# Gate and up weights of an expert: one load each, or two half loads, in a two-block model with a 64-expert layer

## The reference

```python
def swiglu(x, wg, wu, wd):
    return (jax.nn.silu(x @ wg) * (x @ wu)) @ wd
...
    _, idx = lax.top_k(jnp.where(emask, sel, -jnp.inf), TOP_K)     # 6 of 64 experts a token
...
    def block(args):
        tok, w, e = args
        y = swiglu(h[tok], w_gate[e], w_up[e], w_down[e])
        return y * w[:, None]
```

## Time and profile before

| | |
|---|---|
| three runs | 2684.3, 2684.98 (median), 2685.8 us |
| the profiled execution | 2684.57 us, of which 2682.8 are the span from the first to the last instruction |
| what lies around the span | 1.8 us |
| expert stage (first `gate_up` to last down product) | 2075.5 to 2653.4 us of the span |
| PE busy over the whole span | 95% |

### The profile page before, as it was taken

The page is one execution under the profiler, slowest core; times in us unless marked ns, Lnnn a source line. Parts: engine busy times, 40 slices in busy tenths (PEclk is TensorE's granted clock), DMA queues, the critical chain, the costliest instruction groups (busy, mean ns, idle before and its releaser), DMA issues. The chain is left out here.

```text
span 2682.8 us, 30830 instructions
## 1 busy us (share of the span) xinstructions
PE 2557.9 (95%) x10865; PEld 1547.2 (58%) x10865; DVE 1061.1 (40%) x2302; ACT 667.0 (25%) x1319; POOL 600.1 (22%) x539
## 2 busy tenths in 40 slices
PE   8999999999999999999999989999999999999994
PEld 7547888445666478874444537666755443444441
DVE  1126887103333266650023335556623322322226
ACT  2224444202333221210035532222112111111111
POOL 3017887200000144521121001101110111111110
PEclk9999999999999999999989999999998999999997
DMA  4235655532221233232232121110125799999997
GB/s 136 79 94 147 178 161 164 127 87 58 57 56 56 63 94 94 78 90 78 67 87 63 42 52 27 27 32 2 39 84 204 303 419 414 402 389 403 394 393 293
DMA packets 292214, 404.57 MB, mean 151 GB/s; under 512 B 14434, under 2 KB 253752, under 8 KB 267520
## 3 DMA queue, kind: packets, MB, share of 16 engines
q1 hardware_dynamic: 275136, 366.18, 39.6%
q0 software_dynamic: 15632, 34.44, 4.0%
q10 hardware_dynamic: 1328, 2.38, 0.2%
HBM read 396.20 MB, written 27.71 MB: 158 GB/s over the span
## 5 line engine op out<-in xcount | busy, mean ns | idle before, releaser
L947 PE MATMUL bank<-bring 128*128 128x512 f32 x704 | 303.2, 592 | 0.0
L1694 PE MATMUL bank<-bring 128*64 128x512 f32 (+1 forms) x512 | 234.3, 612 | 18.6 <-issue 17.8
L947 PEld LDWEIGHTS bank<-bring 128*128 128x128 f32 x704 | 133.5, 190 | 166.1 <-issue 165.7
L1008 PE MATMUL bank<-ysq 128*128 128x256 f32 x960 | 213.7, 379 | 0.0
L1008 PEld LDWEIGHTS bank<-ysq 128*128 128x128 f32 x960 | 182.4, 190 | 24.8
L2248 DVE TENSOR_TENSOR xT<-bank,xT 128x512 f32<-128x512 f32 x32 | 22.1, 690 | 362.2 <-PE bank L947 362.1
L1008 PE MATMUL bank<-hT,bring 128*128 128x256 f32 x640 | 144.8, 379 | 2.7 <-issue 2.7
L711 POOL TENSOR_TENSOR ysq<-ysq 128x512 f32<-128x512 f32 x23 | 29.3, 1273 | 509.9 <-ACT ysq L1790 443.7
L1694 PEld LDWEIGHTS bank<-bring 128*64 128x64 f32 (+1 forms) x512 | 79.7, 161 | 104.0 <-issue 104.0
L832 POOL TENSOR_TENSOR ffw<-two,maskT 128x512 f32<-128x512 f32 x40 | 53.0, 1329 | 370.5 <-DVE two L2637 316.1
L720 POOL TENSOR_TENSOR two<-two 128x1024 f32<-128x1024 f32 (+2 forms) x72 | 121.2, 1683 | 62.5 <-ACT two L1810 41.6
(11 more groups left out here) (531 smaller groups left out, 4450.6 us busy)
## 6 DMA issues: line engine op xcount, KB each, us to landing
bring<-f_w_in SPq DMA_DIRECT2D x88, 512.0 KB, 5.2
bring<-exp_w_gate SPq DMA_DIRECT2D x32, 1024.0 KB
bring<-exp_w_up SPq DMA_DIRECT2D x32, 1024.0 KB
bring<-exp_w_down SPq DMA_DIRECT2D x32, 1024.0 KB, 20.9
two<-ada_w SPq DMA_DIRECT2D x24, 1024.0 KB, 5.3
bring<-f_w_down SPq DMA_DIRECT2D x16, 1408.0 KB, 7.1
two<-exp_w_gate SPq DMA_DIRECT2D x16, 1024.0 KB, 10.3
two<-exp_w_up SPq DMA_DIRECT2D x16, 1024.0 KB, 19.8
```

Of the source, the lines that this page charges most:

```text
L947: mm = pe.matmul(ps[BANKS[stage][n % 4]][:], w[:, k, n % per * P:(n % per + 1) * P], rhs[:, k, :], start=(k == 0), stop=(k == kb - 1))
L1008: mm = pe.matmul(ps[bank][:, 256 * half:256 * half + 256], weights[:, k, :], rhs[:, k, :], start=(k == 0), stop=(k == 3))
L1694: mm = pe.matmul(ps[3][m * h:m * h + m, :].rearrange("p (m n) -> p m n", m=2), hgT[par][:, k, m * h:m * h + m], w, start=(k == 0), stop=(k ...
```

## The change

Gate and up of an expert are loaded in two halves, of four row blocks each. The half of a matrix is 1024 of the 2048 numbers of each partition, one run of 4 KB in HBM with 4 KB left out behind it. `gate_up` adds one to `exp_gu` after block k = 3 and one after block k = 7, and SP issues the first halves for all experts of a unit when the first count arrives, and the second halves at the second. The down weights are as before. All other waits on `exp_gu` are doubled, so that they end where they ended.

```diff
+            def expert_half(b, e, sem_name, half):
+                for k, n in ((0, "exp_w_gate_2"), (2048, "exp_w_up_2")):
+                    at = slice(1024 * half, 1024 * half + 1024)
+                    sp.dma_start(exw[b][:, k + 1024 * half:k + 1024 * half + 1024], a[n][0][e].rearrange("o r c -> (o r) c")
+                                 .rearrange("(p k) n -> p (k n)", k=KB)[:, at]).then_inc(s(sem_name), 16)
...
-                for q, e in chosen:
-                    sp.wait_ge(s("exp_gu"), u + 1)
-                    expert_in(q % 4, e, sems_of(q), GU)
+                for half in range(2):
+                    for q, e in chosen:
+                        sp.wait_ge(s("exp_gu"), 2 * u + half + 1)
+                        expert_half(q % 4, e, sems_of(q)[0], half)
...
+                    if k == KB // 2 - 1:
+                        half_done(mm)
...
-                    pe.wait_ge(s(f"expgu{q % 4}_loaded"), 32 * (q // 4 + 1))
+                    pe.wait_ge(s(f"expgu{q % 4}_loaded"), 64 * (q // 4 + 1))
...
-                gate_up(par, [q % 4 for q in mine]).then_inc(s("exp_gu"), 1)
+                gate_up(par, [q % 4 for q in mine], lambda mm: mm.then_inc(s("exp_gu"), 1)).then_inc(s("exp_gu"), 1)
...
-                act_e.wait_ge(s("exp_gu"), u + 1)
+                act_e.wait_ge(s("exp_gu"), 2 * u + 2)
```

More of the change, by code:

```diff
@@ L351, in y_loaded @@
                 return loads[n] + 16
-            return 176 + 16 if j == 1 else (32 * EXPERTS // 4 + 16 if n == 0 else 16 * EXPERTS // 4 + 16)
+            return 176 + 16 if j == 1 else (64 * EXPERTS // 4 + 16 if n == 0 else 16 * EXPERTS // 4 + 16)
         def steps_of(stage):
@@ L543, in expert_in, with expert_first @@
                                  .rearrange("(p k) n -> p (k n)", k=rows)).then_inc(s(sem_name), 16)
-            GU, DN = slice(0, 2), slice(2, 3)
+            def expert_half(b, e, sem_name, half):
[3 more added lines that the diff above has]
+                                 .rearrange("(p k) n -> p (k n)", k=KB)[:, at]).then_inc(s(sem_name), 16)
+            DN = slice(2, 3)
+            def expert_first(q, parts):
+                for half in parts:
+                    expert_half(q, bass.ds(q, 1), sems_of(q)[0], half)
             sems_of = lambda q: (f"expgu{q % 4}_loaded", f"expdn{q % 4}_loaded")
             sp.wait_ge(s("rw_y_ready"), 4)
-            expert_in(0, bass.ds(0, 1), sems_of(0), slice(0, 3))
+            expert_first(0, range(2))
+            expert_in(0, bass.ds(0, 1), sems_of(0), DN)
             sp.wait_ge(s("lin_prod"), 5 * KB)
@@ L554, in _ @@
             for q in range(1, 3):
-                expert_in(q, bass.ds(q, 1), sems_of(q), slice(0, 3))
+                expert_first(q, range(2))
+                expert_in(q, bass.ds(q, 1), sems_of(q), DN)
             for k in range(2):
@@ L560, in _ @@
             sp.wait_ge(s("front_stored"), 48)
-            expert_in(3, bass.ds(3, 1), sems_of(3), GU)
+            expert_first(3, range(2))
             sp.wait_ge(s("rt_step"), 8)
@@ L588, in _ @@
             last = len(UNITS) - 1
-            sp.wait_ge(s("exp_gu"), last - 1)
+            sp.wait_ge(s("exp_gu"), 2 * last - 2)
             sp.wait_ge(s("y0_stored"), 16 * (last // 2))
@@ L595, in _ @@
             results_in(1, 0, Y_SEMS[1][0])
-            sp.wait_ge(s("exp_gu"), last)
+            sp.wait_ge(s("exp_gu"), 2 * last)
             results_in(1, 1, Y_SEMS[1][1])
@@ L605, in _ @@
             results_in(4, 0, Y_SEMS[4][0])
-            sp.wait_ge(s("exp_gu"), last + 1)
+            sp.wait_ge(s("exp_gu"), 2 * last + 2)
             results_in(4, 1, Y_SEMS[4][1])
@@ L1686, in shared_down, with gate_up @@
                 mm.then_inc(s("sh_prod"), 1)
-            def gate_up(par, buffers):
+            def gate_up(par, buffers, half_done=lambda mm: None):
                 m = P // len(buffers)
@@ L2171, in rows_turned @@
                 act_e.wait_ge(s("hrow_turned"), 2 * u + half + 1)
-                wait(act_e, s("exp_gu"), u - 1)
+                wait(act_e, s("exp_gu"), 2 * (u - 1))
                 take_rows(u % 2, half).then_inc(s("hgt_ready"), 1)
```

## The result

| | before | after |
|---|---|---|
| median of seven runs | 2684.76 us (2680.97 to 2688.28) | 2694.08 us (2691.99 to 2697.04) |
| profiled execution, its span | 2684.57, 2682.8 us | 2696.26, 2694.5 us |
| last down product begins | 2649.65 us | 2660.84 us |

The ratio is 1.0039 [1.003 to 1.0049], 10.5 us of 2684.76 (8.1 to 13.2; the medians differ by 9.3). Forecast were 2692.2 us, that is 7.2 us more, and a range of 2682 to 2703. The change makes the kernel a little slower, in the stage that was named, and by somewhat more than the sum. Whether the terms of the sum were right is a question of its own: the largest was too small, and the second probably too. The profiled execution of the changed kernel is 2.2 us above its median, so differences between the two profiles, 11 to 12 us, stand somewhat above those of the medians.

The account below looks back on a forecast made before the run. The prediction held the stage from 2130 to 2635 to be bound by the busiest DMA engines. More packets, +9.1, and earlier release, -1.9, summed to +7.2 us, or 2692.2 us, with a range of 2682 to 2703.

Parts of the forecast that it names:

- The bound: Expert stage, 2130 to 2635: as long as the work of the busiest DMA engines.
- The suspicion why some engines have more to do: Expert stage: gathers and scatters leave out empty slots, so they load some DMA engines more than others.
- More packets: Gate and up loads of experts 8 to 63: 18 more packets an expert and engine at 9 ns, +9.1 us.
- half rows are read worse: Gate and up loads: 4 KB rows with gaps cost more, 2709 us; chance 0.15 together with the order costing.
- Earlier release: Last gap before the full stretch, 2126 to 2130: first halves of unit 4 fill it, -1.9 us.
- Order in units of two: Needed second half stands 2.6 us behind the other expert's first half; costed at nothing, as busiest engines have work meanwhile.
- Waits and issues: SP issues two or four more DMAs a unit at some 0.4 us each while idle, and waits are doubled: nothing.
- The tail and what lies before 2075: Outside the expert stage: a sign of being right was that nothing changes there.
- The depth pays: Lows of the expert stage: earlier halves fill them, 2680.3 us, or 2678.4 with the low packet price; chance 0.16.
- part of the price is hidden: 2221 to 2357, where PE is full: 15 experts' packets, 2.4 us, cost nothing; about 2687 us; chance 0.18.
- Each piece pays for itself: The 112 added DMAs: each costs 3.0 us, 336 us together, 3021 us; chance 0.01.

Follow-up runs that it names:

- e10_fewer_bytes: Kernel before, loading only the first half of each gate and up matrix, with the same loads and waits: ratio 0.9877, 33 us faster.
- e9_fill: Kernel before, but in units of one expert the empty slots of partitions 64 to 127 gather row 0, 1294 rows more: ratio 1.0000.
- e12_fill_low: Kernel before, but in units of two experts the first expert's empty slots, partitions 0 to 63, gather row 0, 556 rows more: ratio 1.0034, 9.1 us.
- e5_one_dma: Kernel before, same 1 MB DMAs, but each partition takes two runs of 4 KB, gate and up interleaved by halves in SBUF: ratio 1.0035, 9.4 us.
- e1_late: Changed kernel, but both halves are issued only when gate_up is done, expert by expert; against the kernel before: ratio 1.0061, 16.4 us.
- e4_quarters: Kernel before, but each gate and up load is four DMAs with rows of 2 KB, issued late and matrix by matrix: ratio 1.0094, 25.2 us.
- e11_late_front: Changed kernel, but experts 4 to 9 are issued late, both halves when gate_up is done; against the kernel before: ratio 1.0057.
- e2_order: Changed kernel, but only the first expert's first half is issued early, then its second half, then the other expert; against the kernel before: ratio 1.0041.
- e7_even_odd: Kernel before, but each gate and up load is two DMAs, of even and odd partitions, rows of 8 KB: ratio 1.0009, 2.4 us.
- e3_parts: Kernel before, but each gate and up load is two DMAs, of partitions 0 to 63 and 64 to 127, rows of 8 KB: ratio 1.1612, 430 us slower.

## Why the prediction was right, point by point

**The bound** held. The stage is as long as the transfers (`e10_fewer_bytes`), and it follows the busiest engines and not the mean (`e9_fill` against `e12_fill_low`, but for the rival named there). The prediction took a share of 0.36 for some six engines that stay busy, though it could be sixteen busy for a third of the time. Its reading was right: in the kernel before the number of packets in flight goes down in steps, from 16 at 2389.5 to 11 at 2390, 7 at 2393 and 5 from 2394.5 to SP's next load, all of SP's queue and none of POOL's. This is the window in the last step:

```profile
2394.00:2395.00 1.00, 1.00 (x7) 0.16 (x3) 0.00 (x0) 0.00 (x0) 0.00 (x0) 1.00 0.29 123
```

From 2130 to 2596 the number never falls below five. The low of rows 4 and 5 is there in the changed kernel too. Its SP queue issues nothing between these two rows:

```profile
2388.72 0.38 SPq L542 DMA_DIRECT2D bring<-exp_w_down  x1
2399.54 0.35 SPq L548 DMA_DIRECT2D bring<-exp_w_gate  x1
```

and the share falls to five engines' worth:

```profile
2398.50:2400.50 2.00, 2.00 (x13) 0.65 (x10) 0.00 (x0) 0.00 (x0) 0.00 (x0) 1.00 0.31 129
```

The suspicion why some engines have more to do, that empty slots are left out, is supported by the two fill kernels: more rows cost nothing where the slots are mostly empty. Which engines they are no run shows.

**More packets, +9.1 us,** was sized too small. The number of packets was right (4381 bytes each, 4369 foreseen), and so was the mechanism, but late half loads cost 16.4 us (12.6 to 20.1) and, cut by matrix, 13.7 (9.9 to 17.2). The part that is packet size alone was near: 16 packets an expert at 9 ns over 56 experts are 8.1 us, and `e5_one_dma` measured 9.4. The completion packets, 2 an expert or 1.0 us, measured 2.4 (0 to 4.8). The fixed part of a packet, 9 ns, is what the medians have at every size. The step that failed is taking it for all that a smaller packet can cost, whatever is read beside it: with SP's mean packet and 0.0379 ns a byte it comes out at 8.3 ns in `e5_one_dma`, 10.3 in `e1_late` and 11.8 in the changed kernel, as more packets are slow ones. What makes them slow is not shown. My rival that half rows are read worse named such an effect; what can be left of it is some 5 us against its 16.8 above my sum, and `e4_quarters`, with gaps as well, shows none.

**Earlier release, -1.9 us,** was probably sized too small as well: without it the kernel is 5.9 us slower (1.4 to 10.4), which doesn't exclude the 1.9, and the stage of the profiled execution 2.8. That it acts at the start was right as far as the runs tell (`e11_late_front`). What the sum left out is every gap but the last one ahead of the full stretch. SP's queue in 2118 to 2131 shows the first halves of unit 4 go out 3.4 us ahead of the second ones,

```profile
2123.76 0.33 SPq L548 DMA_DIRECT2D bring<-exp_w_gate  x1
2124.20 0.38 SPq L548 DMA_DIRECT2D bring<-exp_w_up  x1
...
2127.18 0.33 SPq L548 DMA_DIRECT2D bring<-exp_w_gate  x1
```

but the share rises over the whole of 2075 to 2130: the gaps before the last one shrink too, and their work is no longer in the backlog at 2130. I had held that most gaps don't count. Against the late kernel's 0.74 the windows give 4.4 us, of which the last gap is only 4 x (0.99 - 0.69) = 1.2.

**The two errors have opposite signs.** Some 16 less 6 is 10; I had 9.1 less 1.9, 7.2, which lies just under the measured 8.1 to 13.2. That the total came out nearer than its parts was luck.

**Order in units of two: nothing,** confirmed by `e2_order` to within some 4 us. PE's longest waits are at units of two, as foreseen.

**Waits and issues: nothing.** The doubled waits do nothing that a row shows. But many issues don't take 0.4 us any more. In SP's queue, 2363 to 2380 of the changed kernel, they become long:

```profile
2371.08 0.99 SPq L548 DMA_DIRECT2D ysq<-exp_w_up  x1
2372.25 0.38 SPq L548 DMA_DIRECT2D bring<-exp_w_gate  x1
2372.72 7.00 SPq L548 DMA_DIRECT2D bring<-exp_w_up  x1
2379.82 2.13 SPq L542 DMA_DIRECT2D bring<-exp_w_down  x1
```

In the kernel before the same queue has 0.33 to 0.38 us in nearly every issue. No run isolates this. But the sum of all issues on SP's queue in 2130 to 2600 doesn't go with the time: 60 us before, 186 in the changed kernel, 211 in `e5_one_dma`, 250 in `e1_late` and 282 in `e2_order`, which is faster than `e1_late`.

**The tail and what lies before 2075** are as good as unchanged: the last down product begins 11.2 us later, the span is 11.7 us longer. The slower clock behind longer waits, 3.3 us of the 11.2, was in no term of the sum. Whether it costs time of its own where the transfers set the pace, or is covered by them, no run isolates.

**The rivals.** "The depth pays" is excluded: the kernel is slower, the lows are still there, and `e11_late_front` shows no gain from the later units. Against "part of the price is hidden" in 2221 to 2357 speaks that PE loses 5 us there now; the other kernels with half loads lose 2 to 5. "Each piece pays for itself" is excluded by `e7_even_odd`: 112 more DMAs in the stage cost 2.4 us together, 0.02 each. The Trainium skill (DMA: Bandwidth & Descriptors, Anatomy of one DMA) gives a fixed 2.0 us for a DMA that GpSimd issues. On SP's queue, with a backlog, no such part adds up.

## What to carry to other kernels

Where a stage waits for weights, look at whether the DMA engines are out of work or a few of them are behind: a share that goes down in steps and stays at a third in a stretch without issues says the latter, and then smaller pieces add cost and earlier release finds nothing to fill, while fewer bytes help (here taken from all engines; from those behind alone is not tried). Before you cut a transfer for the sake of an earlier start, price both ends apart: the longer packet time over all loads (share x time / bytes of the queue, from one profile), and the DMA work that the idle stretch ahead could really take. Price the usual packet by its median, which gave a fixed 9 ns and 75 ns for each 2 KB here at every size; the mean shows what comes on top. A sum whose terms aren't tested one by one can be right with wrong terms.

## What the runs showed of the hardware that I had not expected

- **Loads into one half of the partitions.** In the same window, 2221 to 2357, loads that each write to 64 neighbouring partitions move 243 GB/s with a full share (`e3_parts`), and loads to every second partition 405 (`e7_even_odd`). POOL's packets beside them slow down as well, by 75%.
- **Issues that take long.** Issues on SP's queue grew from 0.3 to 0.4 us up to 7.00 where loads consist of many packets. `e5_one_dma` has as many DMAs as the kernel before, and in 2363 to 2400 still these:

```profile
2376.82 2.30 SPq L547 DMA_DIRECT2D two<-exp_w_gate  x1
2379.22 3.47 SPq L547 DMA_DIRECT2D two<-exp_w_up  x1
2382.78 2.86 SPq L547 DMA_DIRECT2D ysq<-exp_w_down  x1
```

In 2130 to 2600 the mean issue takes 0.38 us before, 0.57 in `e7_even_odd` with twice the DMAs, and 1.35 in `e5_one_dma` with twice the data packets. It is the number of packets, then, more than that of the DMAs, that lengthens an issue.
